# Sigmoids behind the barrier and a feed-forward on the weighted residual, in a two-block transformer kernel on one core

## The chip, the core and the metric
The kernel runs on one core of a Trainium2 chip. A core has TensorE (PE, the matmuls), VectorE (DVE), ScalarE (ACT), GpSimd (POOL) and SyncE (SP, which only starts transfers here); each runs its own instructions in order, and they wait for each other by semaphores. The metric is the device time of one execution in microseconds, the median of the runs.

## The reference
Two blocks for 256 tokens of width 1024 in fp32: a first one (windowed attention, gated delta rule, an expert layer), which the change does not touch, and a second one whose end it does:

```python
def second_block(x, ...):
    h = rms_norm(x, norm_mix_g)
    proj = h @ w_in
    ...
    yc = diff_attention(...)   # per head: rms_norm(out, subln_g) * (1 - lam_init)
    g = jax.nn.sigmoid(gates + b_gate).reshape(B, S, 3, D_MODEL)
    merged = (g[:, :, 0] * (ya @ w_branch_a)
              + g[:, :, 1] * (yb @ w_branch_b)
              + g[:, :, 2] * (yc @ w_branch_c))
    x = x + merged @ w_out
    h = rms_norm(x, norm_ffn_g)
    u = causal_dwconv(h @ ffn_up, ffn_conv_w, ffn_conv_b)   # three taps over the tokens
    u_gate, u_val = jnp.split(u, 2, axis=-1)
    x = x + (jax.nn.gelu(u_gate) * u_val) @ ffn_down
    return rms_norm(x, final_norm_g)
```

rms_norm divides each token by the root of its mean square and multiplies each of the 1024 channels by a gain. The feed-forward is 2816 wide, 22 blocks of 128, each with a gate and a value.

## The kernel before
Channels lie on the 128 partitions and tokens on the free axis, so x is 8 slices of 128x256. All weights come in one stream of tiles of 128x1024 (512 KB) through a ring of four slots; SP starts a load when the tile that held the slot is used up. The large products are made in three passes: a weight half (128x512) is split by ACT into a rounded high part (`part_hi`, L1278) and by DVE into the rest (`part_lo`, L2288), into one of four buffers of `w_parts`, and the input likewise into `h_parts`; PE multiplies high by high, high by low and low by high. ACT may overwrite a buffer only when PE has used it (`used` waits on half_used or tiles_done, `ahead` then makes the part of tile x + 2).

**End of the second attentions.** 64 tiles of w_in are multiplied by `in2_tile`, the last 24 (the three gates of the merge) interleaved with eight groups g of attention heads: scores, softmax, transposes (`turn2`, L942), weighing (`weigh2`, L953). ACT moves each gate tile out with its bias (`in2_out`, L1435). After the last group (g = 7) comes, on three engines: ACT's sigmoid over the three gate arrays (L1499); DVE's squares and sums of the eight heads of the second attention (L2264, L2265), ACT's root (L1501), DVE's scaling (L2268); then PE turns both attentions' outputs (16 transposes, L977) and ACT moves them out (L1507, L1509). A barrier of all engines (`phase_end`) follows.

**Merge and output.** For each of 8 slices PE multiplies the branches (L990 and L752, two ring tiles), DVE weights them with the gates and adds (L2275 to L2279). Then w_out is multiplied (L752) and DVE adds the residual (L2282, `resid`).

**Feed-forward.** ACT squares each residual slice (L1521), PE sums the squares (L762) and puts the residual, transposed, into the four output banks (L1002). ACT takes the root (L1066), DVE the reciprocal (L1613), then the normed input `h4T` (L1916), ACT its high part (L1408) and DVE its low part (L2083). `ffn_up` (L1018) waits for all of that (h_lo 16). For each block f, `ffn_up` makes two tiles in two of the banks 4 to 7, ACT multiplies by the last tap and adds the bias (`up_out`, L1542), DVE adds the two other taps from the bank (`ff_taps`, L2303 and L2306), ACT takes gelu (L1547), DVE multiplies gate and value (`ff_gate`, L2312), both split the result (`act_parts` L1552, `ff_lo` L2317), and `ffn_down` (L1030) adds its product to the output banks, one block behind. The order of a step is written out by hand in `ff_step` for ACT and for DVE; blocks 2 to 21 of PE are a loop, of the other two blocks 2 to 17. A tile of a step is numbered x: 3f-1 and 3f are the up tiles, 3f+1 the down tile of block f-1.

## Time and profile before

| what | value |
| --- | --- |
| median of 3 runs | 1940.71 us (1940.64 to 1940.84) |
| profiled execution | 1952.05 us, span 1950.3 us |
| PE busy | 1828.4 us, 94% |
| DVE busy | 1231.3 us, 63% |
| ACT busy | 995.5 us, 51% |
| DMA | 283.28 MB, 145 GB/s |
| shares of the chain | PE 82%, DVE 11%, ACT 4% |

A profiled execution is some 11 us longer than the plain ones; sums are made against it. "Busy" is an average over stages. The chain of waits follows the work back from the last instruction and so shows which engine set the time at each moment; the timeline gives single instructions with the idle time before each and what ended it.

### The profile page before, as it was taken

The page shows a single profiled execution, that of the slowest core. Times are in us where ns is not written, and L with a number is a line of the kernel's source. Part 1 is how long each engine was busy: PE and PEld are TensorE (multiplying, and loading weights), DVE is VectorE, ACT ScalarE, POOL GpSimd, SP SyncE. Part 2 cuts the span into 40 slices and gives each one's busy share as a digit, 9 for nine tenths or more (in the row PEclk, how much of TensorE's full clock was granted, in tenths as well). Part 3 has the DMA queues.
Part 4 walks back from the last instruction along what each step waited for, and adds up shares of the span by engine and source line. Part 5 has one row for each costly group of instructions (what it writes and reads, how often), then busy time and mean ns, then how long its engine had stood idle before and what let it go on. Part 6 is the DMA issues. An engine that isn't in the chain of part 4 may idle for free.

```text
span 1950.3 us, 34321 instructions
## 1 busy us (share of the span) xinstructions
PE 1828.4 (94%) x11798; PEld 1637.6 (84%) x11798; DVE 1231.3 (63%) x2461; ACT 995.5 (51%) x1995; POOL 148.7 (8%) x118
## 2 busy tenths in 40 slices
PE   7899999999999976899999999999899997989997
PEld 1777879899889976688999999999899886879997
DVE  1685446556288979766666666666767664237776
ACT  2535623241146668666555555555657554026565
POOL 0000003330064520000000000000000000000000
PEclk9899979899999999999999999999999998989999
DMA  7432212223445520155555555555444332435553
GB/s 264 168 109 95 90 66 98 74 68 131 140 167 178 178 91 1 67 193 193 194 183 191 185 183 191 185 183 193 148 166 163 132 117 86 151 119 184 183 183 118
DMA packets 77267, 283.28 MB, mean 145 GB/s; under 512 B 8576, under 2 KB 8576, under 8 KB 76928
## 3 DMA queue, kind: packets, MB, share of 16 engines
q1 hardware_dynamic: 77184, 282.16, 42.3%
q8 instruction: 53, 0.87, 0.2%
q14 instruction: 30, 0.25, 0.0%
HBM read 281.08 MB, written 1.05 MB: 145 GB/s over the span
## 4 chain that ended last, share of the span: by engine, by line
PE 82%; DVE 11%; ACT 4%; issue 1%; DMA 1%; POOL 1%; PEld 0%; PEldq 0%; ACTq 0%; POOLq 0%; SPq 0%; DVEq 0%
PE banks L823 18%; PE banks L811 16%; PE banks L885 8%; PE banks L430 7%; PE banks L1018 6%; PE banks L752 4%; PE banks L1030 3%; PE banks L609 2%; PE banks L593 2%; DVE split L2018 2%; PE banks L990 1%; PE banks L775 1%; DVE arena L2016 1%; PE banks L401 1%; PE banks L598 1%
## 5 line engine op out<-in xcount | busy, mean ns | idle before, releaser
L1297 ACT ACTIVATE split<-arena 128x512 fp32r<-128x512 f32 x508 | 319.1, 629 | 146.6 <-PE banks L811 83.2
L811 PEld LDWEIGHTS banks<-split 128*128 128x128 f32 x3072 | 379.5, 192 | 11.1 <-DVE split L1955 3.1
L811 PE MATMUL banks<-split 128*128 128x256 f32 x3072 | 383.0, 283 | 3.1 <-DVE split L1955 2.2
L823 PE MATMUL banks<-split 128*128 128x512 f32 x1536 | 365.0, 392 | 2.7 <-issue 2.7
L2032 DVE TENSOR_TENSOR split<-arena,split 128x512 fp32r<-128x512 f32 x412 | 281.6, 690 | 117.0 <-ACT split L1297 111.4
L823 PEld LDWEIGHTS banks<-split 128*128 128x128 f32 x1536 | 284.4, 189 | 58.8 <-issue 2.9
L1278 ACT ACTIVATE split<-arena 128x512 fp32r<-128x512 f32 x264 | 163.9, 626 | 85.2 <-PE banks L885 29.8
L885 PE MATMUL banks<-split 128*128 128x256 f32 x1344 | 169.3, 286 | 4.0 <-DVE split L2114 3.9
L885 PEld LDWEIGHTS banks<-split 128*128 128x128 f32 x1344 | 164.7, 193 | 7.6 <-issue 5.9
L430 PE MATMUL banks<-split 128*128 128x256 f32 (+2 forms) x936 | 154.0, 327 | 8.1 <-DVE split L1619 7.1
L430 PEld LDWEIGHTS banks<-split 128*128 128x128 f32 (+1 forms) x936 | 137.3, 200 | 26.4 <-issue 8.3
L1018 PEld LDWEIGHTS banks<-split 128*128 128x128 f32 x1056 | 132.0, 195 | 8.9 <-DVE split L2083 7.3
L1018 PE MATMUL banks<-split 128*128 128x256 f32 x1056 | 132.6, 286 | 7.1 <-DVE split L2083 7.1
L2091 DVE TENSOR_TENSOR split<-arena,split 128x512 fp32r<-128x512 f32 x128 | 87.3, 690 | 70.5 <-ACT split L1278 69.0
L2288 DVE TENSOR_TENSOR split<-arena,split 128x512 fp32r<-128x512 f32 x132 | 89.2, 688 | 47.8 <-ACT split L1278 46.2
L849 PE MATMUL banks<-split,arena 128*128 128x128 f32 x512 | 67.0, 286 | 31.6 <-DVE arena L2021 31.6
L2416 POOL TENSOR_TENSOR split<-arena,split 128x512 fp32r<-128x512 f32 x68 | 90.7, 1360 | 71.9 <-DVE split L1955 51.2
L849 PEld LDWEIGHTS banks<-split,arena 128*128 128x128 f32 x512 | 62.0, 198 | 36.6 <-DVE split L2018 32.5
L752 PE MATMUL banks<-arena 128*128 128x256 f32 x384 | 86.3, 385 | 3.7 <-DVE arena L2279 2.2
L752 PEld LDWEIGHTS banks<-arena 128*128 128x128 f32 x384 | 74.0, 193 | 14.7 <-DVE arena L2279 2.6
L1619 DVE TENSOR_TENSOR split<-arena,split 128x512 fp32r<-128x512 f32 x78 | 52.9, 689 | 48.9 <-ACT split L1073 48.7
L2048 DVE TENSOR_TENSOR arena<-arena 128x256 f32<-128x256 f32 x80 | 49.1, 614 | 45.0 <-ACT arena L1359 44.9
(375 smaller groups left out, 2378.4 us busy)
## 6 DMA issues: line engine op xcount, KB each, us to landing
arena<-wstream SPq DMA_DIRECT2D x525, 512.0 KB, 3.2
arena<-x_t SPq DMA_DIRECT2D x1, 2048.0 KB, 13.1
arena<-matsa SPq DMA_DIRECT2D x1, 1234.0 KB, 6.2
out_t<-arena SPq DMA_DIRECT2D x4, 256.0 KB, 2.1
arena<-mats SPq DMA_DIRECT2D x1, 576.0 KB, 8.0
arena<-crow SPq DMA_DIRECT2D x1, 512.0 KB, 7.0
arena<-rows SPq DMA_DIRECT2D x1, 512.0 KB, 4.8
arena<-mats SPq DMA_DIRECT2D x1, 449.0 KB, 3.9
```

The costliest lines, as they stand in the source:

```text
L430: mm = pe.matmul(ps[0:rows, b, 0:m], w_parts[:, c, (2 * t + k // 4) % 4, P * (k % 4):P * (k % 4) + rows], hp[:, e, k, 0:m], start=(k == 0 ...
L752: mm = pe.matmul(ps[:, b, 0:S], w[:, P * k:P * k + P], src[:, k, :], start=(k == 0), stop=(k == KT - 1))
L811: mm = pe.matmul(ps[:, 4 + b, 0:S], w_parts[:, c, (2 * m + half) % 4, P * k:P * k + P], h_parts[:, e, 4 * half + k, :], start=(half == 0 a ...
L823: mm = pe.matmul(ps[:, 2 * tt + half, :], g_parts[:, e, j % 2, P * tt:P * tt + P], w_parts[:, c, (2 * m + half) % 4, :], start=(first and ...
L849: pe.matmul(ps[:, W_BANKS[g % 3] + t // 4, P * (t % 4):P * (t % 4) + P], hot1[g % 2][:, t, :], hot2[:, g % 2, t, :].bitcast(F32), start=Tr ...
L885: mm = pe.matmul(out, w_parts[:, c, (2 * m + half) % 4, P * k:P * k + P], src[:, e, 4 * half + k, :], start=(half == 0 and k == 0 and c + ...
L1018: mm = pe.matmul(ps[:, 4 + 2 * (f % 2) + m, 0:S], w_parts[:, c, (2 * (M_FFN + x) + half) % 4, P * k:P * k + P], h_parts[:, e, 4 * half + k ...
L1278: act.activation(w_parts[:, 0, h % 4, :], ring[:, slot, 512 * half:512 * half + 512], ACT.Copy).then_inc(sem["w_hi"], 1)
L1297: act.activation(w_parts[:, 0, (2 * m + half) % 4, :], ring[:, peer_slot(m), 512 * half:512 * half + 512], ACT.Copy).then_inc(sem["w_hi"], 1)
L2032: dve.tensor_tensor(w_parts[:, 1, (2 * m + half) % 4, :], ring[:, slot, 512 * half:512 * half + 512], w_parts[:, 0, (2 * m + half) % 4, :] ...
L2288: dve.tensor_tensor(w_parts[:, 1, h % 4, :], ring[:, tile_of(M_FFN + x) % RING, 512 * half:512 * half + 512], w_parts[:, 0, h % 4, :].bitc ...
L2416: pool.tensor_tensor(w_parts[:, 1, (2 * m + half) % 4, :], ring[:, (N_PEER + m) % RING, 512 * half:512 * half + 512], w_parts[:, 0, (2 * m ...
```

## The change
At the end of the attentions the sigmoids move behind the barrier, in four pieces, each over the same two slices of the three gates, with a new semaphore gates2_ready for the merge on DVE; a square root of one number (for its table) stands in the last group and another behind the sigmoids. The first attention's output is turned in the last group, between tiles 61 and 62, six of the eight head sums are made there too, and the scaling is in two halves, each with its four transposes, now into banks 4 and 5. In the feed-forward the input of `ffn_up` is the residual times the gain (ACT's high part from L1530, DVE's low part `weighted_lo`), and the reciprocal root multiplies the product instead: `ff_norm` on DVE copies the bank, times the root, to `upn` in SBUF, from which ACT and DVE take the taps. PE may reuse the bank after `ff_norm` instead of after the taps. The sum of squares stands between the first two up tiles and the transposed residual after the second. In a step ACT makes the second half's weight part before the last tap instead of after it.

```diff
-        h4T = buf("h4T", KT, S)
-        upp = buf("upp", 2, 2, S + 2)
+        upn = buf("upn", 2, 2, S)
...
+            def turn_heads(m, qt, b):
+                for f in range(4):
+                    mm = pe.transpose(ps[:, b, P * f:P * f + P], o2[m][:, qt, P * f:P * f + P], ident)
+                mm.then_inc(sem["o_turned"], 1)
...
+                if g == 7:
+                    pe.wait_ge(sem["logits2"], 32)
+                    for qt in range(2):
+                        turn_heads(0, qt, qt)
...
-            pe.wait_ge(sem["o2_ready"], 1)
-            for m in range(2):
-                for qt in range(2):
-                    for f in range(4):
-                        mm = pe.transpose(ps[:, 2 * m + qt, P * f:P * f + P], o2[m][:, qt, P * f:P * f + P], ident)
-                    mm.then_inc(sem["o_turned"], 1)
+            pe.wait_ge(sem["weighted"], 16 + 24)
+            for qt in range(2):
+                pe.wait_ge(sem["o2_ready"], qt + 1)
+                turn_heads(1, qt, 4 + qt)
...
-            sum_squares2(4, sq3, 3)
-            for tt in range(2):
+            def turn_residual(tt):
...
-            pe.wait_ge(sem["h_lo"], 16)
-
-
-
-            def ffn_up(f, i4=0):
-
-                for m in range(2):
...
+                if f >= 2:
+                    pe.wait_ge(sem["ff_norm"], 2 * i4 + 2 * f - 3 + m)
...
+                if x == 0:
+                    pe.wait_ge(sem["resid"], 2 * KT + 5)
...
+                        if x == 0:
+                            pe.wait_ge(sem["h_lo"], 12 + 4 * half + k + 1)
...
-            ffn_up(0)
-            ffn_up(1)
+            ffn_up(0, 0)
+            sum_squares2(4, sq3, 3)
+            ffn_up(0, 1)
+            for tt in range(2):
+                turn_residual(tt)
+            for m in range(2):
+                ffn_up(1, m)
             ffn_down(0)
             with pe.Fori(0, (FT - 2) // 4) as i:
                 for f in range(2, 6):
-                    ffn_up(f, 4 * i)
+                    for m in range(2):
+                        ffn_up(f, m, 4 * i)
                     ffn_down(f - 1, 4 * i)
...
+                if g == 7:
+                    act.activation(small[:, 84:85], eps, ACT.Sqrt)
+                    for qt in range(2):
+                        act.wait_ge(sem["o_turned"], 2 + qt + 1)
+                        act.activation(o2T[0][:, :, P * qt:P * qt + P], bank(qt, 4, P), ACT.Copy).then_inc(sem["o_moved"], 1)
...
+                else:
+                    act.wait_ge(sem["o2_stat"], 1)
+                    act.activation(vec[:, 40:48], vec[:, 40:48], ACT.Sqrt, bias=eps, scale=1.0 / P).then_inc(sem["o2_root"], 1)
                 in2_out(42 + 3 * g)
-            for c in range(3):
-                act.wait_ge(sem["proj_free"], 4 + 39 + 40 + 8 * c + 8)
-                act.activation(g2T[:, 8 * c:8 * c + 8, :], g2T[:, 8 * c:8 * c + 8, :], ACT.Sigmoid)
-            act.wait_ge(sem["o2_stat"], 1)
-            act.activation(vec[:, 40:48], vec[:, 40:48], ACT.Sqrt, bias=eps, scale=1.0 / P).then_inc(sem["o2_root"], 1)
-            for m in range(2):
-                for qt in range(2):
-                    act.wait_ge(sem["o_turned"], 2 + 2 * m + qt + 1)
-                    dst = o2T[m][:, :, P * qt:P * qt + P]
-                    if m == 0:
-                        o = act.activation(dst, bank(qt, 4, P), ACT.Copy)
-                    else:
-                        o = act.activation(dst, bank(2 + qt, 4, P), ACT.Identity, scale=vec[:, 48:49])
-                    o.then_inc(sem["o_moved"], 1)
+            for qt in range(2):
+                act.wait_ge(sem["o_turned"], 4 + qt + 1)
+                act.activation(o2T[1][:, :, P * qt:P * qt + P], bank(4 + qt, 4, P), ACT.Identity, scale=vec[:, 48:49]).then_inc(sem["o_moved"], 1)
...
+            branch_gates = g2T.rearrange("p (m k) s -> p m k s", m=3)
+            for k in range(0, KT, 2):
+                act.activation(branch_gates[:, :, k:k + 2, :], branch_gates[:, :, k:k + 2, :], ACT.Sigmoid).then_inc(sem["gates2_ready"], 1)
+            act.activation(small[:, 84:85], eps, ACT.Sqrt)
...
+                act.activation(h_parts[:, 0, k, :], res[:, k, :], ACT.Identity, scale=col("norm_ffn2")[:, k:k + 1]).then_inc(sem["h_hi"], 1)
                 act.activation(sq3[:, k, :], res[:, k, :], ACT.Square).then_inc(sem["squares"], 1)
-            roots(4, S, 3)
-            act.wait_ge(sem["normed"], 2)
-            act_hi(h4T)
...
-                act.activation(upc[:, f % 2, m, :], ps[:, 4 + 2 * (f % 2) + m, 0:S], ACT.Identity, scale=last_tap[:, c],
+                act.wait_ge(sem["ff_norm"], 2 * i4 + 2 * f + m + 1)
+                act.activation(upc[:, f % 2, m, :], upn[:, f % 2, m, :], ACT.Identity, scale=last_tap[:, c],
...
                 used(x, 0, i4)
                 ahead(x, 0, i4)
                 used(x, 1, i4)
+                ahead(x, 1, i4)
                 act_parts(f - 1, i4)
                 up_out(f, 0, i4)
-                ahead(x, 1, i4)
                 used(x + 1, 0, i4)
                 ahead(x + 1, 0, i4)
                 used(x + 1, 1, i4)
+                ahead(x + 1, 1, i4)
                 up_out(f, 1, i4)
-                ahead(x + 1, 1, i4)
...
                     used(x, half)
-                    if half:
-                        up_out(0, x)
                     ahead(x, half)
+                if x == 0:
+                    roots(4, S, 3)
+            for m in range(2):
+                up_out(0, m)
...
+            def head_squares(h0, h1):
+                link(dve.tensor_tensor(head_sq[:, h0:h1, :], heads[:, h0:h1, :], heads[:, h0:h1, :], ALU.mult))
+                return dve.tensor_reduce(vec[:, 40 + h0:40 + h1], head_sq[:, h0:h1, :], AX, ALU.add)
...
+                if g == 7:
+                    dve.wait_ge(sem["o_scaled"], 11)
+                    head_squares(0, 6)
...
-            heads = o2[1].rearrange("p a (b c) -> p (a b) c", b=4)
-            tmp = flat(lg[:, 0, :, :]).rearrange("p (a b) -> p a b", a=8)
-            link(dve.tensor_tensor(tmp, heads, heads, ALU.mult))
-            dve.tensor_reduce(vec[:, 40:48], tmp, AX, ALU.add).then_inc(sem["o2_stat"], 1)
+            head_squares(6, 8).then_inc(sem["o2_stat"], 1)
             dve.wait_ge(sem["o2_root"], 1)
             link(dve.reciprocal(vec[:, 40:48], vec[:, 40:48]))
-            dve.tensor_tensor(heads, heads, bc(vec[:, 40:48], 2, P), ALU.mult).then_inc(sem["o2_ready"], 1)
+            for qt in range(2):
+                h = heads[:, 4 * qt:4 * qt + 4, :]
+                dve.tensor_tensor(h, h, bc(vec[:, 40 + 4 * qt:44 + 4 * qt], 2, P), ALU.mult).then_inc(sem["o2_ready"], 1)
...
+                if d % 2 == 0:
+                    dve.wait_ge(sem["gates2_ready"], d // 2 + 1)
...
+            def weighted_lo(k):
+                dve.wait_ge(sem["h_hi"], 12 + k + 1)
+                dve.scalar_tensor_tensor(h_parts[:, 1, k, :], res[:, k, :], col("norm_ffn2")[:, k:k + 1], h_parts[:, 0, k, :].bitcast(F32),
+                                         ALU.mult, ALU.subtract).then_inc(sem["h_lo"], 1)
...
-            def part_lo(x, i4=0):
-
+                if d:
+                    weighted_lo(d - 1)
+                if d == 6:
+                    for half in range(2):
+                        part_lo(0, half)
+            weighted_lo(KT - 1)
...
-            for x in range(2):
-                part_lo(x)
-            norm(4, h4T, res, col("norm_ffn2")).then_inc(sem["normed"], 1)
-            dve_lo(2, h4T)
+                    part_lo(x, half)
+            inverse(4, S)
...
+            def ff_norm(f, m, i4=0):
+
+                dve.wait_ge(sem["tiles_done"], 3 * i4 + N_FFN + max(3 * f - 1, 0) + m + 1)
+                dve.tensor_tensor(upn[:, f % 2, m, :], ps[:, 4 + 2 * (f % 2) + m, 0:S], rstd[:, 0:S], ALU.mult).then_inc(sem["ff_norm"], 1)
...
-                part_lo(3 * f + 1, i4)
+                part_lo(3 * f + 1, 0, i4)
+                ff_norm(f, 0, i4)
+                part_lo(3 * f + 1, 1, i4)
                 ff_lo(f - 1, i4)
                 ff_taps(f, 0, i4)
-                part_lo(3 * f + 2, i4)
+                part_lo(3 * f + 2, 0, i4)
+                ff_norm(f, 1, i4)
+                part_lo(3 * f + 2, 1, i4)
                 ff_taps(f, 1, i4)
...
             for m in range(2):
-                part_lo(2 + m)
+                ff_norm(0, m)
+            for half in range(2):
+                part_lo(3, half)
+            for m in range(2):
                 ff_taps(0, m)
```

PE at the end of the attentions, before; L885 are tiles of w_in (24 matmuls each), L977 the transposes of the outputs, L990 the merge:

```order
L885 MATMUL banks<-split 128x256 x72
L942 MATMUL banks<-arena 128x128 x4
L953 MATMUL banks<-arena 128x128 x4
L885 MATMUL banks<-split 128x256 x24
L977 MATMUL banks<-arena 128x128 x16
L990 MATMUL banks<-arena 128x256 x8
```

and after (L884, L958 and L996 are the same three):

```order
L884 MATMUL banks<-split 128x256 x48
L958 MATMUL banks<-arena 128x128 x8
L884 MATMUL banks<-split 128x256 x24
L941 MATMUL banks<-arena 128x128 x4
L952 MATMUL banks<-arena 128x128 x4
L884 MATMUL banks<-split 128x256 x24
L958 MATMUL banks<-arena 128x128 x8
L996 MATMUL banks<-arena 128x256 x8
```

Eight of the sixteen transposes moved in front of the last two tiles.

DVE from the residual on, before; L2282 is the residual, L2288 weight parts, L1916 the norm, L2083 the low part of the input:

```order
L2282 TENSOR_TENSOR arena<-banks,arena 128x256 [waits tiles_done] x8
L2288 TENSOR_TENSOR split<-arena,split 128x512 [waits w_hi] x4
L1613 RECIPROCAL arena<-arena 128x256 [waits roots]
L1916 SCALAR_TENSOR_TENSOR arena<-arena 128x256 [waits dve_chain]
L1916 SCALAR_TENSOR_TENSOR arena<-arena 128x256 x7
L2083 TENSOR_TENSOR split<-arena,split 128x512 [waits h_hi] x4
L2288 TENSOR_TENSOR split<-arena,split 128x512 [waits w_hi] x2
L2303 SCALAR_TENSOR_TENSOR arena<-banks,arena 128x255 [waits ff_out]
```

and after, from the last residual slices on (L2301 is the residual, L2296 the weighted low part, L2291 weight parts, L2318 ff_norm):

```order
L2296 SCALAR_TENSOR_TENSOR split<-arena,split 128x256 [waits h_hi]
L2291 TENSOR_TENSOR split<-arena,split 128x512 [waits w_hi] x2
L2301 TENSOR_TENSOR arena<-banks,arena 128x256 [waits tiles_done]
L2296 SCALAR_TENSOR_TENSOR split<-arena,split 128x256 [waits h_hi] x2
L2291 TENSOR_TENSOR split<-arena,split 128x512 [waits w_hi] x4
L1622 RECIPROCAL arena<-arena 128x256 [waits roots]
L2318 TENSOR_TENSOR arena<-banks,arena 128x256 [waits tiles_done,dve_chain]
L2318 TENSOR_TENSOR arena<-banks,arena 128x256 [waits tiles_done]
```

The norm and the split behind the reciprocal are gone; the low part stands by each residual slice, and three tiles' weight parts stand before the reciprocal.

ACT in step 1 (the loop's order is the same), before; L1278 are weight parts, L1552 the gated high part, L1542 the last tap:

```order
L1278 ACTIVATE split<-arena 128x512 [waits slot1_loaded,half_used]
L1552 ACTIVATE split<-arena 128x256 [waits ff_act,tiles_done]
L1542 ACTIVATE arena<-banks,arena 128x256
L1278 ACTIVATE split<-arena 128x512 [waits slot1_loaded]
L1278 ACTIVATE split<-arena 128x512 [waits slot2_loaded,half_used]
L1542 ACTIVATE arena<-banks,arena 128x256 [waits tiles_done]
L1278 ACTIVATE split<-arena 128x512 [waits slot2_loaded]
L1547 ACTIVATE arena<-arena 128x256 [waits ff_conv]
```

and after (L1289, L1559, L1549):

```order
L1289 ACTIVATE split<-arena 128x512 [waits slot1_loaded,half_used]
L1289 ACTIVATE split<-arena 128x512 [waits slot1_loaded,tiles_done]
L1559 ACTIVATE split<-arena 128x256 [waits ff_act]
L1549 ACTIVATE arena<-arena 128x256 [waits ff_norm]
L1289 ACTIVATE split<-arena 128x512 [waits slot2_loaded,half_used]
L1289 ACTIVATE split<-arena 128x512 [waits slot2_loaded,tiles_done]
L1549 ACTIVATE arena<-arena 128x256 [waits ff_norm]
L1554 ACTIVATE arena<-arena 128x256 [waits ff_conv]
```

Weight parts stand in pairs now, and the last tap waits for ff_norm instead of for the tile.

## Rows read from the trace of the kernel before

**Rows 1.** Windows: us; busy PE, PEld, DVE, ACT, POOL; PE clock; DMA share, GB/s.
```profile
1751.00:1753.00 2.00, 2.00 (x11) 2.00 (x11) 0.50 (x1) 0.30 (x1) 0.00 (x0) 0.50 0.00 0
1762.00:1933.00 171.00, 171.00 (x1199) 160.74 (x1198) 125.96 (x241) 103.99 (x200) 0.00 (x0) 1.00 0.52 178
```

**Rows 2.** Chain that ended last, feed-forward: start us, us, engine and line.
```profile
1734.89 3.47 PE banks L762 x16
...
1761.68 3.00 PE banks L1030 x12
1764.68 5.75 PE banks L1018 x48
1770.43 2.84 PE banks L1030 x12
```

**Rows 3.** The same chain at the end of the second attentions.
```profile
1629.73 2.89 PE banks L885 x24
...
1633.20 1.28 ACT L1499
1634.49 5.51 ACT arena L1499 x3
...
1641.87 1.23 DVE arena L2268
1643.15 3.69 PE banks L977 x16
1646.86 0.69 ACT arena L1509
1647.64 3.72 PE banks L990 x16
```

**Rows 4.** Timeline of PE, last group: start us, us, line, shape, [idle before, releaser].
```profile
1618.80 8.88 PE L885 MATMUL banks<-split 128*128 128x256 f32 x72
...
1628.58 1.16 PE L953 MATMUL banks<-arena 128*128 128x128 f32 x8 [0.46 <-ACT arena L1492]
```

**Rows 5.** Timeline of PE, start of the feed-forward.
```profile
1738.18 1.91 PE L1002 MATMUL banks<-arena 128*128 128x128 f32 x16
1747.18 14.35 PE L1018 MATMUL banks<-split 128*128 128x256 f32 x96 [7.09 <-DVE split L2083]
```

**Rows 6.** Timeline of ACT, end of the second attentions.
```profile
1625.20 0.62 ACT L1278 ACTIVATE split<-arena 128x512 fp32r<-128x512 f32 x1
...
1641.30 0.30 ACT L1501 ACTIVATE arena<-arena 128x8 f32<-128x8 f32 x1
```

**Rows 7.** Timeline of DVE, end of the second attentions.
```profile
1626.72 0.68 DVE L2091 TENSOR_TENSOR split<-arena,split 128x512 fp32r<-128x512 f32 x1
1629.77 0.42 DVE L2255 COPY arena<-banks 128x256 f32<-128x256 f32 x1 [2.37 <-PE banks L953]
1630.23 1.23 DVE L2264 TENSOR_TENSOR arena<-arena 128x1024 f32<-128x1024 f32 x1
```

**Rows 8.** Timeline of DVE, feed-forward: residual, reciprocal, gated low part.
```profile
1734.92 0.42 DVE L2282 TENSOR_TENSOR arena<-banks,arena 128x256 f32<-128x256 f32 x1 [3.03 <-PE banks L752]
...
1738.88 1.75 DVE L1613 RECIPROCAL arena<-arena 128x256 f32<-128x256 f32 x1 [1.13 <-ACT arena L1066]
...
1769.70 0.42 DVE L2317 TENSOR_TENSOR split<-arena,split 128x256 fp32r<-128x256 f32 x1
```

**Rows 9.** Timeline of ACT, last square of the residual.
```profile
1735.38 0.42 ACT L1521 ACTIVATE arena<-arena 128x256 f32<-128x256 f32 x1 [2.00 <-DVE arena L2282]
```

**Rows 10.** Groups by line and shape, 1762 to 1933 us: busy, mean ns, idle before.
```profile
L2303 DVE SCALAR_TENSOR_TENSOR arena<-banks,arena 128x255 f32<-128x255 f32 x41 | 19.6, 477 | 0.0
```

**Rows 11.** Timeline of PE, the last down tile.
```profile
1937.67 3.06 PE L1030 MATMUL banks<-split 128*128 128x512 f32 x12 [1.56 <-DVE split L2317]
```

**Rows 12.** Timeline of PE, the first and the second output product.
```profile
491.16 27.89 PE L752 MATMUL banks<-arena 128*128 128x256 f32 x128 [1.44 <-DVE arena L1907]
...
1705.38 29.50 PE L752 MATMUL banks<-arena 128*128 128x256 f32 x128 [2.23 <-DVE arena L2279]
```

More of the change, by code:

```diff
@@ L72 @@
 rgw_in rg_in rg_conv_done rg_gates rg_sig rg_coeff rg_mult rg_ln rg_steps h3_ready rg_exp rg_pow rg_square lam_exp
-logits2 probs2 maps2 o2_stat o2_root o2_ready ff_out ff_conv ff_taps ff_gelu ff_act final_done""".split()
+logits2 probs2 maps2 gates2_ready o2_stat o2_root o2_ready ff_norm ff_out ff_conv ff_taps ff_gelu ff_act final_done""".split()
 def build(nc, wstream, x_t, cols_in, mats_in, mats1_in, matsa_in, crow_in, rows_in, out):
@@ L1404, in part_hi @@
                 tile_hi(n % RING, 12 * i4 + 16 * (n // RING + 1), half, 2 * m + half)
-            def act_hi(src):
-                for c in range(4):
-                    act.activation(h_parts[:, 0, 2 * c:2 * c + 2, :], src[:, 2 * c:2 * c + 2, :], ACT.Copy).then_inc(sem["h_hi"], 1)
             for k in range(KT):
@@ L1911, in _ @@
                                          ALU.mult, ALU.add).then_inc(sem["resid"], 1)
-            def norm(r, dst, src, gain):
-                inverse(r, S)
-                for k in range(KT):
-                    o = dve.scalar_tensor_tensor(dst[:, k, :], src[:, k, :], gain[:, k:k + 1], rstd[:, 0:S], ALU.mult, ALU.mult)
-                return o
             def route_query(h):
@@ L2078, in _ @@
             step(127, last=True)
-            def dve_lo(r, src):
-                for c in range(4):
-                    dve.wait_ge(sem["h_hi"], 4 * r + c + 5)
-                    dve.tensor_tensor(h_parts[:, 1, 2 * c:2 * c + 2, :], src[:, 2 * c:2 * c + 2, :],
-                                      h_parts[:, 0, 2 * c:2 * c + 2, :].bitcast(F32), ALU.subtract).then_inc(sem["h_lo"], 1)
             def in2_lo(t, half):
```

44 lines of the change are left out of this document (24 added, 20 removed).

## The prediction, made before the changed kernel ran

> **What bounds the kernel now.** I read the chain of waits first. From the last part of the second attentions to the end it is mostly TensorE (PE), with three places where PE stands still, and these are where the diff works. The windows view gives the other half: in the 171 us of the feed-forward loop PE is busy all the time at full clock while DVE is busy 125.96 us and ACT 103.99 us [rows 1]. So whatever shortens other engines inside the loop gains nothing; only the idle stretches of PE, and the clock that it loses by them, can be won. In a step of the loop PE does two up tiles in 5.75 us and one down tile in 2.84, together 8.59 [rows 2].
>
> **Part A, the end of the attentions.** PE ends tile 63 at 1632.6 and begins the merge at 1647.64 [rows 3]. Between them stand, one behind the other: a table load of 1.28, the three sigmoids of 5.51, a second table load, a small square root, DVE's scaling of the heads, 1.23, sixteen transposes in 3.69 and the last ACT move of 0.69 [rows 3]. The change takes the sigmoids behind the barrier, puts one square-root table load, half the transposes and six of eight head sums into the last group, and halves the scaling. My schedule:
> - PE's first eight transposes stand after tile 61. Tiles 60 to 62 are the 72 matmuls from 1618.80, the last two thirds ending at 1624.8 and 1627.7 [rows 4]. At full clock sixteen such transposes take 1.91 [rows 5], so eight cost 0.96, and all that follows on PE comes 0.96 later: tile 62 at 1628.6, the weighing after its 0.46 wait [rows 4] ends at 1630.7, tile 63 at 1633.6.
> - ACT is free at 1625.8 [rows 6]; table load 1.28 and the dummy root, 0.30 as the small root [rows 6], end at 1627.4, two moves of 512 columns, at most the 0.69 of [rows 3] each, by 1628.7. Tile 62's eviction starts at 1628.7, so they just fit.
> - DVE is free at 1627.4, after its last weight part. A copy of 256 columns takes 0.42, the product of 1024 1.23 [rows 7]; they make 1.05 ns per column: six heads (768) 0.96 for the product, the like for the sum, done at 1629.3, before the weighing ends. After it: copy 0.42, product 0.42, sum 0.41 (1632.0), ACT's root 0.30, the reciprocal 0.27 (from the root's end to the scaling at 1641.87 [rows 3, 6]), first half of the scaling 0.69: 1633.3, the second at 1634.0. Tile 63 is the later, by 0.2.
> - PE transposes 1633.6 to 1634.1 and 1634.1 to 1634.6; ACT moves 0.69 each to 1635.45, barrier 0.1: the merge starts at 1635.55. **Gain 12.1 us.**
> The sigmoids cost nothing behind the barrier if the merge finds them done. Three of 2048 columns take 5.51, so one of the four new ones (1536 columns) takes 1.38; with the table load the first is done 2.7 us after the barrier and the last at 6.8. DVE needs the first after two PE tiles of 3.45, at 6.9, and then two pairs of tiles pass for each. The square-root load after them ends at 8.1, and ACT's next work is tens of us off.
>
> The row on the price of a table load: the sigmoid's load begins at 1633.20 and its first activation at 1634.49 [rows 3], so the load costs 1.28 and no more. The Trainium skill (ScalarE: Activation LUTs, "What ACT_TABLE_LOAD costs") has a drain of about 1.38 us beside each load, some 2.66 together. That rule speaks against putting the load in the last group: by it ACT would be late for tile 62's eviction by about 1.4 us, and the sum would be 1.4 us smaller. The trace speaks for the smaller price.
>
> **Part B, the start of the feed-forward.** PE ends the output product at 1734.89 and starts the first down tile at 1761.68, 26.79 us [rows 2]. PE's own work in it is four up tiles at 2.87 (half of 5.75), the sum of squares 3.47 [rows 2] and the transposes of the residual 1.91 [rows 5], together 16.87 at full clock. The other 9.92 are 7.09 of waiting for root, reciprocal (1.75, [rows 8]), norm and split [rows 5], and 2.8 that the up tiles lose at half clock (0.50 at 1751 to 1753 [rows 1]: 14.35 for 96 matmuls [rows 5] against 11.5). The change removes the norm from in front of the up tiles (the weighted residual goes in; the root multiplies the product). Is PE fed without a gap?
> - Residual tile 7 is written by DVE from 1734.92, 0.42 [rows 8], ACT's high part takes 0.42 from 1735.38 (the square stands there now [rows 9]), DVE's low part 0.48 as the tap, an operation of the same kind [rows 10]: ready at 1736.3. PE started at 1734.89 and reaches the eighth slice after 7 x 0.36, at 1737.4. Slack 1.1. Its weight parts follow DVE's residual slice 6 (3.45 before slice 7) and a low part, 0.68 each: 1733.8.
> - PE: up tile 0 to 1737.8, sums of squares to 1741.2, up tile 1 to 1744.1, transposes to 1746.0, up tiles 2 and 3 to 1748.9 and 1751.7.
> - Root on ACT at 1741.7, reciprocal on DVE to 1743.5, the two ff_norm at 0.42 to 1744.7, two weight parts to 1746.0, four taps at 0.48 to 1747.8, gate 1748.2, weight part 4, ff_norm, weight part, and the low part of the gated tile at 1750.8. Gelu's table load lies under the taps. PE wants it at 1751.7: slack 1.0.
> So nothing is waited for: the first down tile starts at 1751.7. **Gain 9.9 us.**
>
> **Part C, the loop.** Added for each step: two DVE products from PSUM, 0.42 each as the residual's sum [rows 8], so DVE goes from 125.96 to about 143 of 171. Taps and ACT's last tap read SBUF instead of PSUM; I leave the taps' 0.48 unchanged [rows 10]. Each ff_norm waits for an up tile, with a weight part and the taps queued behind it on DVE; ACT's last tap waits for ff_norm, with weight parts and gelu behind. Times from a step's start on PE (0), with some 0.2 for each signal from PE: ACT's weight parts 4 end at 2.2 and 3.8 (they now stand ahead of the last tap), the gated high part at 4.1, last tap 4.5. DVE: gate 1.5 to 1.9, part 2.9, ff_norm 3.05 to 3.5, part 4.45, gated low part 4.8, taps 5.7, part 6.3, ff_norm 6.65, part 7.35, taps 8.25, part 8.85, part (which waits for ACT at 9.4) 10.1, which is 1.5 of the next step: the cycle closes. PE wants the gated low part at 5.75, so 1.0 is spare. Now that part begins at 1769.70 and lasts 0.42, against the down tile's start at 1770.43 [rows 2, 8]: 0.3 spare. The loop is PE's before and after. **0 us**, with no gain possible from above.
>
> **Part D, the tail.** PE waits 1.56 before the last down tile [rows 11], which so starts 8.59 + 1.56 = 10.15 after its step's start. By the times of part C the last gate ends at 8.7, ACT's high part 9.15 (it waits for the down tile's end), the low part 9.6. **Gain 0.6 us**, from 0.2 to 1.0.
>
> Sum: 12.1 + 9.9 + 0.0 + 0.6 = 22.6. The profiled execution took 1952.05 (span 1950.3), 11.34 over the median 1940.71 of the plain runs; it would come to 1929.4, and the median to **1918.1 us**.
>
> **The rivals.**
> - *Clock at the merge's end.* Before the output product PE waits 2.23 us and the 128 matmuls then take 29.50; the same 128 after a wait of 1.44 earlier in the kernel take 27.89 [rows 12]. The difference, 1.6, is half-clock time. The work there is unchanged, but it comes 12 us sooner, and if the clock holds the result is 1916.5. The Trainium skill (TensorE: Matmul & The Clock Gate, "What's actually happening") says that activity is judged on a beat that is not reset by the kernel, so that one and the same pause may or may not cost. Chance 0.22.
> - *ACT late in the last group*, if the load holds ACT twice its 1.28 us, or the clock halved after the barrier's 1 us pause, at the 1.6 of the rival above: 1.3 to 1.6 lost, 1919.4 to 1919.7. Against the latter: pauses of such a length before (the 1.44 of [rows 12]) did not halve it. 0.11.
> - *Feed-forward start not gapless*: down to half of the clock and wait gain lost, 3 to 5 us, if a part of the chain in B is 1 us later than I have it: 1922. For it: only 1.0 of slack. 0.06.
> - *Part A's gain not real*: the sigmoids are only moved and DVE waits for them at the merge, 5.51 and a load lost again: 1924.9. It needs the first pair 4.2 us later than worked out. 0.03.
> - *Slower: the added waits close a longer cycle in the loop.* If each DVE wait in a step costs more than the 1.0 of slack, the cycle grows on DVE and ACT, 21 times. A step 0.3 longer gives 6 us, 1924.4 (0.05). From 1.1 us more per step on (9.7 against 8.59, that is the gated low part at 6.9 instead of 4.8) it eats the whole gain; at 1.3 it gives 1918.1 + 27.3 = 1945.4. Against it: DVE would have 7.2 us of work in 8.59. 0.03.
>
> **How the numbers follow.** Forecast 0.50 at 1918.1; the clock rival 0.22, the late ACT 0.11: the range from 1915.0 to 1921.5 takes these in (the clock rival with the tail's best end below, the forecast with both small losses above) and leaves about 0.17 out. Faster by over 0.2% (3.9 us, about what a measurement of this kernel can tell from no change) are all but the slower rival and a sliver: 0.96; within 0.01; slower 0.03.
>
> **What would show it.** The profile after should have PE waits of at most 1 us between tile 63 and the merge, sigmoid rows under the first merge tiles, transposes in the last group at 0.12 each, no half clock in the first up tiles, 17 us from the output product's end to the first down tile, and steps of 8.59. It is wrong if a DVE or ACT row ends waits of PE inside the loop, if gates end DVE's wait at the merge, or if PE's wait before the first down tile exceeds 1 us.

## The result, and the profile after

The changed kernel takes 1921.23 us (median of 4 runs, 1917.66 to 1923.58), the kernel before beside it 1940.78 (1940.64 to 1944.05). The ratio is 0.9878, with a 95% interval from 0.985 to 0.9906: 1.2% faster. The profiled execution took 1921.18 us, its span is 1919.4.

Single executions of one and the same kernel lie up to 15 us apart here (the kernel before: 1936.61 to 1951.75), so I read the result by stages of the chain of waits rather than by the total. The profile is one more such execution and not longer for being profiled: 1921.18 lies among the plain runs, and a second profile of the kernel before took 1938.78. Its first one, 1952.05, was a long execution; the 11 us that I put down to profiling were that. Each number is the distance between the starts or ends of two groups on PE:

| stage, us | before | after | predicted gain | gain |
| --- | --- | --- | --- | --- |
| end of tile 63 to the merge, with 0.85 for the transposes moved ahead of it | 15.02 | 1.98 | 12.1 | 12.2 |
| merge | 57.74 | 57.74 | 0 | 0 |
| output product, 128 matmuls | 29.50 | 27.89 | 0 (1.6 in the rival) | 1.61 |
| its end to the first down tile | 26.80 | 16.70 | 9.9 | 10.10 |
| first to last down tile | 175.99 | 173.95 | 0.6 | 2.04 |
| last down tile to the end of the span | 12.63 | 13.03 | 0 | -0.40 |

Together 25.5 us. The two profiled executions differ by 30.9; the other 5.4 lie ahead of tile 63, in code that the change doesn't touch. The medians differ by 19.6 only. The -0.40 of the last row is not the change's: from the last down tile to the end of DVE's last instruction are 10.08 us before and 10.04 after, and what follows, 2.55 and 2.99, is the last output transfer, which took 3.7 in a repeat of the kernel after.

The chain that ended last, kernel after, end of the attentions (start us, us, what; L958 are transposes, L996 the merge's first branches):

```profile
1625.24 2.87 PE banks L884 x24
1628.11 0.60 PE banks L958 x4
1628.71 0.02 issue
1628.73 0.69 ACT arena L1514
1629.42 0.62 ACTq L377
1630.09 3.72 PE banks L996 x16
```

This answers to [rows 3]: table load, sigmoids, second load, root and scaling are gone from the chain. What stands between tile 63 and the merge is four transposes, two ACT moves and the barrier. Where the sigmoids went, and whether the table load makes ACT late, shows in the timeline of ACT (the releaser of an idle time in brackets), and of DVE in the last row:

```profile
1620.48 1.28 ACT L1495 ACT_TABLE_LOAD   x1
1621.78 0.20 ACT L1495 ACTIVATE arena<-arena 128x1 f32<-128x1 f32 x1
1621.89 1.07 ACT L1498 ACTIVATE arena<-banks 128x512 f32<-128x512 f32 x2
1623.28 0.47 ACT L1442 ACTIVATE arena<-banks,arena 128x256 f32<-128x256 f32 x1 [0.33 <-PE banks L884]
...
1630.10 1.28 ACT L1519 ACT_TABLE_LOAD   x1
1631.40 5.60 ACT L1519 ACTIVATE arena<-arena 128x1536 f32<-128x1536 f32 x4
...
1637.36 0.42 DVE L2282 TENSOR_TENSOR arena<-banks,arena 128x256 f32<-128x256 f32 x1 [8.83 <-PE banks L751]
```

ACT waits 0.33 for tile 62, not the other way round, so it was not late. From the start of the load to the small root are 1.30 us, and nothing else lies between them. DVE's first merge product waits for PE (L751), while the first of the four sigmoids ended near 1632.8.

The start of the feed-forward, same chain (L761 sums of squares, L1007 transposes of the residual, L1023 up tiles, L1035 down tiles):

```profile
1687.83 27.89 PE banks L751 x128
1715.73 2.88 PE banks L1023 x24
1718.61 3.45 PE banks L761 x16
1722.06 2.87 PE banks L1023 x24
1724.93 1.75 PE banks L1007 x16
1726.68 5.75 PE banks L1023 x48
1732.42 2.75 PE banks L1035 x12
1735.17 5.75 PE banks L1023 x48
1740.92 2.75 PE banks L1035 x12
```

Every row starts where the one before ends, and no up tile runs at half clock (2.87 for 24; the 96 matmuls of [rows 5] took 14.35). A step is 8.50 us, where [rows 2] give 8.59: the down tile takes 2.75 instead of 2.84. The windows view of the same 171 us of the loop (us; PE, PEld, DVE, ACT, POOL busy; PE clock) beside [rows 1]:

```profile
1735.00:1906.00 171.00, 170.17 (x1201) 159.99 (x1199) 142.43 (x282) 107.77 (x200) 0.00 (x0) 1.00 0.53 175
```

DVE is at 142.4 us, as forecast (143).

### The profile page after: what moved, and what is told of

Read it like the earlier page. It is cut to its first block, busy times and chain, and to the rows that moved or that the text cites. A ratio compares the mean times of both kernels' runs of the same rounds, so it can differ in the third digit from the quotient of the medians.

```text
span 1919.4 us, 34464 instructions
## 1 busy us (share of the span) xinstructions
PE 1815.5 (95%) x11798; PEld 1626.8 (85%) x11798; DVE 1246.2 (65%) x2504; ACT 1001.6 (52%) x2003; POOL 148.7 (8%) x118
## 3 DMA queue, kind: packets, MB, share of 16 engines
HBM read 281.08 MB, written 1.05 MB: 147 GB/s over the span
## 4 chain that ended last, share of the span: by engine, by line
PE 84%; DVE 10%; ACT 3%; issue 1%; POOL 1%; DMA 0%; PEld 0%; PEldq 0%; ACTq 0%; POOLq 0%; SPq 0%; DVEq 0%
PE banks L822 18%; PE banks L810 16%; PE banks L884 8%; PE banks L429 7%; PE banks L1023 6%; PE banks L751 4%; PE banks L1035 3%; PE banks L608 2%; PE banks L592 2%; DVE split L2021 2%; PE banks L400 2%; PE banks L996 1%; PE banks L774 1%; DVE arena L2019 1%; PE banks L597 1%
## 5 line engine op out<-in xcount | busy, mean ns | idle before, releaser
L1289 ACT ACTIVATE split<-arena 128x512 fp32r<-128x512 f32 x264 | 164.7, 628 | 109.9 <-PE banks L1023 52.3
L884 PE MATMUL banks<-split 128*128 128x256 f32 x1344 | 169.5, 286 | 4.0 <-DVE split L2110 3.9
L884 PEld LDWEIGHTS banks<-split 128*128 128x128 f32 x1344 | 164.7, 193 | 7.6 <-issue 5.9
L1023 PEld LDWEIGHTS banks<-split 128*128 128x128 f32 x1056 | 129.7, 192 | 1.7
L1023 PE MATMUL banks<-split 128*128 128x256 f32 x1056 | 130.8, 283 | 0.0
L2291 DVE TENSOR_TENSOR split<-arena,split 128x512 fp32r<-128x512 f32 x132 | 89.1, 688 | 15.3 <-ACT split L1289 15.3
L751 PE MATMUL banks<-arena 128*128 128x256 f32 x384 | 84.7, 380 | 3.7 <-DVE arena L2286 2.2
L751 PEld LDWEIGHTS banks<-arena 128*128 128x128 f32 x384 | 72.8, 190 | 14.3 <-DVE arena L2286 2.6
```

The source lines that it names most:

```text
L751: mm = pe.matmul(ps[:, b, 0:S], w[:, P * k:P * k + P], src[:, k, :], start=(k == 0), stop=(k == KT - 1))
L884: mm = pe.matmul(out, w_parts[:, c, (2 * m + half) % 4, P * k:P * k + P], src[:, e, 4 * half + k, :], start=(half == 0 and k == 0 and c + ...
L1023: mm = pe.matmul(ps[:, 4 + 2 * (f % 2) + m, 0:S], w_parts[:, c, (2 * (M_FFN + x) + half) % 4, P * k:P * k + P], h_parts[:, e, 4 * half + k ...
L1289: act.activation(w_parts[:, 0, h % 4, :], ring[:, slot, 512 * half:512 * half + 512], ACT.Copy).then_inc(sem["w_hi"], 1)
L2291: dve.tensor_tensor(w_parts[:, 1, h % 4, :], ring[:, tile_of(M_FFN + x) % RING, 512 * half:512 * half + 512], w_parts[:, 0, h % 4, :].bitc ...
```

## The experiments

The stages of the runs that compare them (us; "again" are repeats of the same kernel):

| | before | before again | before, padded | A alone | B alone | after | after again | merge early |
| --- | --- | --- | --- | --- | --- | --- | --- | --- |
| tile 63 to merge | 15.02 | 15.01 | 17.54 | 1.97 | 15.02 | 1.98 | 1.98 | 1.98 |
| merge | 57.74 | 57.75 | 57.74 | 57.75 | 57.75 | 57.74 | 57.75 | 56.56 |
| product | 29.50 | 29.46 | 29.58 | 27.89 | 29.50 | 27.89 | 27.89 | 27.89 |
| to first down tile | 26.80 | 26.77 | 26.82 | 26.81 | 16.69 | 16.70 | 16.70 | 16.69 |
| first to last down tile | 175.99 | 175.99 | 175.98 | 175.99 | 173.95 | 173.95 | 173.94 | 173.94 |
| last down tile to end | 12.63 | 12.56 | 12.59 | 12.54 | 12.64 | 13.03 | 13.81 | 12.57 |

**Part A alone** (the attention end and the merge of after, the feed-forward of before).

> The kernel before with only the end of the attentions changed (transposes, head sums and root in the last group, sigmoids behind the barrier). Theory: tile 63's end to the merge's start shrinks from 15.0 to about 2.8 us, a gain of 12.1 to 12.2 against the kernel before after the 0.96 for the transposes, and nothing else moves: the wait before the first down tile and the 26.8 us from the output product's end to it stay. Median about 1928.5. Rival (the gain is given back at the merge, DVE waiting for the sigmoids): the merge takes more than its 57.7 us, by up to 6.9. Second rival (the 1.6 us at the output product was a gain of this part): its 128 matmuls take 27.9 here and 29.5 in a kernel without this part, always; if the clock's fall there is chance, it comes either way.

Measured: 1931.82 us against 1945.22, ratio 0.9933 (0.9903 to 0.9962). **Part B alone** (the feed-forward of after, the rest of before).

> The kernel before with only the feed-forward changed. Theory: output product's end to the first down tile 16.7 us instead of 26.8 (gain 10.1), the loop's step 8.50 instead of 8.59 (gain 1.7 over 20 steps), the wait before the last down tile 1.2 instead of 1.56; together 12.1, median about 1928.6. Rival (the parts overlap, or each needs the other, since the clock carries over from one idle stretch to the next): less than 11 alone, and the sum of both parts below the joint gain of the two stages, 24.

Measured: 1937.37 us, ratio 0.9958 (0.9938 to 0.9978). The product of the two ratios is 0.9891, within the interval of the whole change, and the gains by stages add up: the parts are independent as far as this shows. The medians missed both expectations. Part A gained 13.4 us against the kernel beside it, where its stages give 13.8, but part B gained 7.9 where its stages give 12.1. Only one execution of each has a trace, so whether B's other executions were long in the part ahead of tile 63, and by chance, stays open. The stages put the gains where the prediction had them, and two surprises each with one part: the product's clock comes with A, the step of 8.50 with B. The chain, first of A alone, then of B alone:

```profile
1689.67 27.89 PE banks L752 x128
...
1770.30 2.83 PE banks L1037 x12
1778.88 2.84 PE banks L1037 x12
```

```profile
1704.82 29.50 PE banks L751 x128
...
1768.01 2.75 PE banks L1028 x12
1776.51 2.75 PE banks L1028 x12
```

**The order of ACT's step.** In the kernel after, the second weight part stands behind the last tap again, as before the change:

```diff
                 used(x, 1, i4)
-                ahead(x, 1, i4)
                 act_parts(f - 1, i4)
                 up_out(f, 0, i4)
+                ahead(x, 1, i4)
                 used(x + 1, 0, i4)
                 ahead(x + 1, 0, i4)
                 used(x + 1, 1, i4)
-                ahead(x + 1, 1, i4)
                 up_out(f, 1, i4)
+                ahead(x + 1, 1, i4)
```

> The changed kernel with ACT's step in the old order: the last tap ahead of the second half's weight part. What made the loop's step 8.50 instead of 8.59? Theory (the gated low part now comes 1.1 us before PE wants it, where it came 0.3 before, and PE loads it as weights ahead of time): here the low part ends only some 0.1 to 0.2 before it is wanted, and the step is 8.59 or more. Rival (the taps no longer read PSUM banks beside PE): the step stays 8.50.

Measured: 1945.91 us in one execution, and a step of 9.98. The expectation missed, and so did its rival. With this one hunk undone more than the whole gain is gone: from the output product's end to the end of the span are 234.5 us, 30.8 more than the 203.7 of the kernel after, where the change gains 25.5 in all. Timelines of PE (down tile), DVE (ff_norm L2318, then a weight part L2291) and ACT (last tap L1549, gated high part L1559):

```profile
1805.77 3.00 PE L1035 MATMUL banks<-split 128*128 128x512 f32 x12 [1.24 <-DVE split L2339]
...
1802.79 0.42 DVE L2318 TENSOR_TENSOR arena<-banks,arena 128x256 f32<-128x256 f32 x1
1804.61 0.69 DVE L2291 TENSOR_TENSOR split<-arena,split 128x512 fp32r<-128x512 f32 x1 [1.40 <-ACT split L1289]
...
1802.31 0.42 ACT L1559 ACTIVATE split<-arena 128x256 fp32r<-128x256 f32 x1 [1.42 <-DVE arena L2334]
1803.45 0.60 ACT L1549 ACTIVATE arena<-arena 128x256 f32<-128x256 f32 x1 [0.73 <-DVE arena L2318]
1807.85 0.60 ACT L1549 ACTIVATE arena<-arena 128x256 f32<-128x256 f32 x1 [2.75 <-DVE arena L2318]
```

The ring can be read off: ACT's last tap waits for DVE's ff_norm (0.73, 2.75), ACT makes the weight part only behind the tap, DVE's next weight part waits for it (1.40), and the gated low part behind that is what PE waits for (1.24). DVE and ACT hand to each other in series and leave room: in 185 us of this loop DVE is busy 129.35 and ACT 95.38. This is the forecast's slower rival, at the step (9.7 and more) where it said that the gain is eaten. In the kernel after, the weight part stands ahead of the tap, and DVE waits 0.24 for the one that it makes behind ff_norm, instead of 1.40:

```profile
1806.75 0.69 DVE L2291 TENSOR_TENSOR split<-arena,split 128x512 fp32r<-128x512 f32 x1 [0.24 <-ACT split L1289]
```

The kernel before had the old order too, and DVE waited 1.59 there ahead of the gated low part. Without ff_norm that wait closed no ring, but it made the low part late, as the next runs show.

**How much room is on DVE.** One or two needless DVE products of 768 columns (0.95 us) in each step, ahead of the gated low part:

```diff
+                dve.tensor_tensor(h3T[:, 0:3, :], x2T[:, 0:3, :], x2T[:, 3:6, :], ALU.add)
+                dve.tensor_tensor(h3T[:, 3:6, :], x2T[:, 0:3, :], x2T[:, 3:6, :], ALU.add)
```

> The changed kernel with one added DVE sum of 768 columns (0.95 us, unused) in each step ahead of the low part of the gated tile. In the changed kernel that part ends 1.0 to 1.1 us before PE wants it. Theory (spare of 1.0, and the shorter step is due to the earlier low part, which PE loads ahead): PE still does not wait, the step is 8.50 to 8.59, nearer to 8.59 since the part is late again. Rival (the 0.09 came from taps that no longer read PSUM): 8.50 to 8.51. Rival (DVE's and ACT's waits close a longer cycle, as with the old order of ACT, where the step was 9.99): 9 us or more.

> The same with two such sums (1.90 us in each step). Theory: DVE's work is 7.4 + 1.9 = 9.3 us in a step, more than PE's 8.5, so DVE is the bound and the step is 9.3 us and what it still waits for ACT, 9.5 to 10.3: 20 to 35 us over the changed kernel, which is the slower kernel of the forecast. Rival (PE's spare hides it): under 9.0.

Measured: 1920.62 us with one (step 8.61), 1935.71 with two (step 9.49). One, then two, each with the low part (L2339) and the down tile (L1035) that follows it:

```profile
1805.00 0.95 DVE L2348 TENSOR_TENSOR arena<-arena 128x768 f32<-128x768 f32 x1
1805.87 0.41 DVE L2339 TENSOR_TENSOR split<-arena,split 128x256 fp32r<-128x256 f32 x1
1806.41 3.01 PE L1035 MATMUL banks<-split 128*128 128x512 f32 x12
```

```profile
1809.87 0.42 DVE L2339 TENSOR_TENSOR split<-arena,split 128x256 fp32r<-128x256 f32 x1
1810.42 3.01 PE L1035 MATMUL banks<-split 128*128 128x512 f32 x12 [0.72 <-DVE split L2339]
```

In the kernel after the low part ends 1.0 before the down tile (1807.36 + 0.42 against 1808.76 in the timeline), and the down tile takes 2.91. With one product it ends 0.13 before, PE shows no wait, and the down tile takes 3.01. PE did wait all the same. The tile's weight loads (PEld) fetch the gated input, and `ffn_down` waits for its low part ahead of them all. They start, in the kernel before, with one product, and in the kernel after, at:

```profile
1770.25 2.60 PEld L1030 LDWEIGHTS banks<-split 128*128 128x128 f32 x12
```

```profile
1806.41 2.59 PEld L1035 LDWEIGHTS banks<-split 128*128 128x128 f32 x12
```

```profile
1808.64 2.60 PEld L1035 LDWEIGHTS banks<-split 128*128 128x128 f32 x12
```

Where the profile books a wait for the low part (two products, and ACT's old order) the first weight load starts 0.12 to 0.13 us after the low part's end. In the kernel before (1769.70 + 0.42 to 1770.25) and with one product (1805.87 + 0.41 to 1806.41) it starts at the same 0.12 to 0.13, step after step, so there too it started as soon as the low part let it. In the kernel after it starts 0.86 after the low part, and 0.12 ahead of the tile's own first matmul. So the 0.1 per step that the change gained unforecast is a short wait for the low part that the kernel before had in each step and that the profile books as nothing. The rival that the taps no longer read PSUM does not hold: with one product they read SBUF, and the step is 8.61. That the earlier low part of the kernel after comes from ACT's order is read from the two waits above; the kernel before with that order alone was not run. A second product costs nearly its length: it adds 0.88 to the step.

**The small square roots** (both left out: the table is loaded by the root that needs it).

> The changed kernel without the two square roots of one number. The table loads then stand directly before the real roots, but a load was seen to run while ACT waits. Theory: the load in the last group runs after the two turned copies, 1624.3 to 1625.6 on the changed kernel's clock, before the head sums are ready at 1626.6, and the load for the sum of squares runs during the merge: nothing changes, merge starts within 0.1 us of the same place. Rival (the load waits for the operand): 1.3 us later at the merge's start, and 1.3 later root in the feed-forward, of which the slack of 1 us before the first down tile hides most.

Measured: 1924.93 us, gap 1.97, every other stage as after. The two small roots are worth nothing: the table load goes ahead of the root's wait for DVE and lies in ACT's idle time anyway.

**Sigmoids ahead of the barrier again**, in the otherwise changed kernel:

> The changed kernel with the four sigmoid pieces (and the small root behind them) ahead of the barrier, behind ACT's last move: the rest of the end of the attentions stays changed. Theory: the sigmoids' table load, 5.6 us of sigmoids and the second load with its root come between the last move and the barrier, so tile 63's end to the merge's start grows from 2.0 to about 10.4, and the rest of the kernel is as it was; of the 12.2 us of this part 8.3 are then the sigmoids' and 3.9 the rest's. Rival (PE's first merge tiles also run at half clock after the longer pause): 1.5 to 1.7 us more in the merge's first tile.

Measured: gap 10.39 us, 1928.3 us in one execution. The chain:

```profile
1625.76 1.26 ACT arena L1514 x2
1627.02 0.02 issue
1627.04 1.28 ACT L1518
1628.32 0.01 issue
1628.33 1.48 ACT arena L1518
1629.81 5.67 ACTq L377
1635.52 5.37 PE banks L996 x16
```

The gap grows by 8.4 us: the sigmoids with their load (1.28 and 5.60) and the second load with its small root (1.28 and 0.20). The other 3.8 of A's 12.2 us are the rearranged last group; this run and the kernel before both have two table loads in this stretch. The long pause also halves the clock at the merge's start (5.37 for 16 matmuls that take 3.72 after): 1.65 us more, which the stage table of the kernel before doesn't show, since its transposes took that loss (3.69 in [rows 3]).

**The merge's first products one tile earlier.** DVE waits for the first branch tile, and for the second only before it needs it:

```diff
-                dve.wait_ge(sem["tiles_done"], N_BR2 + 2 * d + 2)
+                dve.wait_ge(sem["tiles_done"], N_BR2 + 2 * d + 1)
...
+                dve.wait_ge(sem["tiles_done"], N_BR2 + 2 * d + 2)
                 dve.tensor_tensor(t, ps[:, b + 1, 0:S], g2T[:, 8 + d, :], ALU.mult)
```

> The changed kernel with DVE's merge split: its first three operations start when the first of the two PE tiles of a slice is done, only the last two wait for the second. Theory: behind the last merge tile two operations of 0.85 us stand instead of five of 2.1, PE's pause before the output product falls from 2.2 to about 0.9: merge's start to output product 56.4 instead of 57.7, all later stages alike; 1.3 us, less than the spread of the runs. Rival (DVE's reads from the bank beside PE's writes, or the added waits, cost as much): 57.5 or more.

> The merge's two first products one tile earlier, as in e7. Stage by stage the trace of e7 gives 1.17 us (merge 56.57 instead of 57.74 us), and all else equal. Theory: median 1.2 us below that of the changed kernel beside it, within their spread, so the two may not be told apart by time; merge 56.57 again. Rival: the time of e7 (1915.8) was the real size, 5 us below.

> The changed kernel again, beside the next one, for its spread. Theory: the product clock holds again (128 matmuls in 27.89 us) and no stage between tile 63 and the end moves by 0.05 us; the whole time still differs by up to 5 us between executions, by half-clock stretches in the unchanged first part. Rival (the product clock is chance): 29.5 us in some profiles, this one perhaps. Time: 1916 to 1924 us.

Measured: 1915.78 us (1911.81 to 1925.02, ratio 0.9875) and, in the second set, 1917.33 (1911.86 to 1922.76), beside it the changed kernel 1922.8 (1913.86 to 1926.34). PE waits 1.05 before the output product instead of 2.23 [rows 12], the merge is 56.56:

```profile
1679.41 4.80 PE L751 MATMUL banks<-arena 128*128 128x256 f32 x21 [1.05 <-DVE arena L2287]
```

By the stages this version is 1.2 us faster than the changed kernel, and up to the last down tile nothing else moves. The medians say 5.5, but the ranges overlap nearly whole, and the traces show no more than 1.2 that the edit can explain (the last transfer, 0.5 to 1.2 shorter, is the one that varies anyway).

**The product's clock.**

> The kernel before, once more, for one row: the 128 matmuls of the output product. If the half clock there is chance from execution to execution they take 27.89 now with fair odds; if it belongs to the kernel (its pauses and their distances) 29.5 again. I expect 29.5 (two of two so far without part A, none of eight with it). Gap tile 63 to merge 15.02, merge 57.7.

> The kernel before with two needless products of 1024 columns on DVE (1.23 us each) ahead of the reciprocal at the end of the attentions: PE idles 2.5 us longer there, and nothing else changes. Gap 17.5 us. If the half clock at the product is set by how long ago the pause at the merge was, it stays (that distance, 57.7 us, is unchanged): 29.5. If it is set by the moment alone, the product, 2.5 us later, may take anything from 27.9 to 31, most likely not 29.50.

Measured: 29.46 and 29.58 us. The half clock at the output product thus came in all four profiles without part A (before, before again, padded, B alone) and in none of the ten with it; the pause ahead of the product is 2.2 us in all but the two with the early merge. It is no chance of one execution. Nor does it belong to the long pause before the merge alone: with the sigmoids ahead of the barrier that pause is 9.3 us and halves the clock, the distance to the product is 59.4 us, and the product still took 27.89. Which part of A decides stays open; shifting by 2.5 us (padded) didn't end it. One rival is left untested: that the distance from the earlier pause decides. Merge and product start 57.7 us apart in the four profiles with the half clock and 59.4 in the one that had the long pause without it, and no run varies that distance alone.

The two profiles of the unchanged kernel differ by 13.3 us in span, and by 13.2 already at the end of tile 63 (1632.62 and 1619.46). In windows of a quarter of a microsecond PE's clock is 0.5 for 78.5 us of the first 1600 in one and 54.8 in the other; half of the difference is 11.9. One such stretch, before and before again:

```profile
246.00:270.00 24.00, 23.94 (x92) 17.98 (x90) 5.76 (x9) 3.84 (x7) 0.00 (x0) 0.57 0.12 42
```

```profile
246.00:270.00 24.00, 21.53 (x128) 19.26 (x127) 10.42 (x22) 8.38 (x19) 0.00 (x0) 0.79 0.12 44
```

## Why the prediction was right, and where it was not

- **Part A, 12.1 predicted, 12.2 measured.** The gap was worked out as 1.95 us (1633.6 to 1635.55) and is 1.98. The steps in it held, too: ACT was in time for tile 62 by 0.33 (predicted: just), and the first half of the scaling came 0.24 before tile 63's end; the second came at 1628.52, 0.4 after it, while PE turned the first (predicted: 0.3 before and 0.4 after). The sigmoids were free, DVE waits for PE at the merge. Part A alone gave the same gap, and the sigmoids put back took 8.4 of it away. The Trainium skill (ScalarE: Activation LUTs, "What ACT_TABLE_LOAD costs") would have made ACT late by its drain; the trace doesn't agree, with 1.30 us from the load's start to the next activation and the load right behind other work with the sigmoids put back (1627.02 to 1627.04).
- **Part B, 9.9 predicted, 10.1 measured.** The chain without gaps came as listed (16.87 predicted, 16.70 measured), and so did the clock. The last link: low part of the gated tile 1.0 before it is wanted by the prediction, 1.14 in the trace (1730.86 + 0.42 to 1732.42). That the first up tiles keep the clock was right because PE never stops.
- **Part C, the step that failed.** It said "0 us, with no gain possible from above". The working of the cycle was right: 1.0 of spare, where the chain has 1.1 (1773.36 + 0.42 to 1774.92). What failed is the other reading, "0.3 spare" in the kernel before, and with it the claim that PE stood nowhere for another engine in the loop. That spare was taken to the chain's start of the down tile, 1770.43; its first weight load started at 1770.25, 0.13 after the low part's end, which is the lag of a tile that waits. There was no spare but a wait of some 0.1 in each step, and it was to be won: some 1.7 of the 2.04 us between first and last down tile. The sign was 2.84 for the down tile, which I took for its own length; it takes 2.75.
- **Part D, 0.6 predicted, 0.36 measured** (PE's wait before the last down tile 1.20 instead of 1.56). The mechanism was right and the size off. The last low part ends 9.66 us after its step's start on PE (9.6 predicted); it was the 10.15 of before that I had too long, the chain has 10.08.
- **The clock at the output product.** The rival at 0.22 was the case that came, in every profile with part A. I priced it rightly (1.6 predicted, 1.61 measured) and gave it too small a chance, because I saw it as luck. The Trainium skill (TensorE: Matmul & The Clock Gate, "What's actually happening") has a beat that the kernel does not reset; by it one and the same kernel could show both. In the first 300 us the traces agree with that (0.57 and 0.79 above). At the output product no kernel showed both: four of four and none of ten. Why is not shown.
- **The slower rival.** I argued against it from busy time (7.2 of 8.59 on DVE). That was not the reason it didn't come: with the two lines of ACT's order undone DVE has the same work and the step is 9.98. I had listed the order in the working of part C, but took it as one of several details; it is the condition on which ff_norm costs nothing.
- **The sum.** Terms of 22.6 against 25.5 by stages, and yet the median came out 3.1 us above the forecast. The forecast started from three runs of the kernel before within 0.2 us; beside the result its median was 1940.78, but beside the experiments 1939.25, 1945.22 and 1946.42. The means of all recorded runs (1943.8 before, 1920.95 for ten of the kernel after) differ by 22.8, still 2.7 under the stages, and no run shows where those went. The range of 1915.0 to 1921.5 was made of terms of the change, with nothing for the start value or for the spread of the untouched first part, which alone is more than that. So the stages bear the forecast out, but that the median fell inside, 0.3 under the upper end, was partly luck: two gains of 1.6 and some 1.7 that the sum had at nothing were hidden by that spread, and six later runs of the same kernel had a median of 1922.8.

## What to carry to other kernels

When a new hand-over between two engines goes into a step that both share, look first at what is queued behind the receiver: work that the sender needs next must stand ahead of the wait. That one order was worth 1.5 us a step here, more than all the operations added. And where single executions differ by 13 us in code that no one touched, compare stages between two fixed places of the chain; up to the last down tile they repeat within about 0.1 us.

## What the runs showed of the hardware

- A matmul group that waits for an operand from DVE starts its first weight load 0.12 to 0.13 us after DVE's end. A wait of some 0.1 us shows in no idle time, only in this lag and in the length of the group (3.01 against 2.91 in the timeline).
- A square root of 128x1 on ACT takes 0.20 us, a sigmoid of 128x1536 1.40, and a table load 1.28 whether work stands right ahead of it or not.
- The half clock after a pause lasted about 10 us at the merge (1637.0 to 1647.25 before, 1628.6 to 1638.9 with the sigmoids put back) and 3.2 us at the output product (1705.4 to 1708.7), by the granted clock in the windows view. After equal pauses of 2.23 us it came in one kernel and not in the other.
